# Head rows duplicated into both tile halves: one transfer with a repeated source in place of two

## What is computed

```python
def hybrid_layer(x, ...):                      # twice
    z = rms_norm(x, norm_g) @ w_in
    o_a = fox_attention(heads(fq, 4), heads(fk, 4), heads(fv, 4), ff + fox_b) * silu(f_gate)
    o_b = conformer_conv(...)
    o_c = nsa_attention(heads(nq, 8), ..., heads(nks, 2), heads(nvs, 2), heads(nkw, 2), heads(nvw, 2), ...)
    return x + concatenate([o_a, o_b, o_c]) @ w_out

def second_block(x, ...):                      # two layers
        h = rmsnorm(x, norm1_g[l]) @ w_in[l]
        y_a = gdn_mixer(a_qkv, a_z, a_ab, ...)
        y_b = diff_mixer(b_q, b_k, b_v, ...)   # s = q k^T per head of 64, softmax, a = p0 - lam * p1
        y_c = swa_mixer(c_q, c_k, c_v, ...)
        y_d = mlstm_mixer(d_q, d_k, d_v, d_if, d_o, ...)
        ...
```

## Time and profile before

| | |
|---|---|
| median of 3 runs | 4367.03 us (4355.88 to 4370.16) |
| the profiled execution | 4360.56 us, of which the span of the profile is 4358.8 us |
| TensorE matmul busy | 3567.8 us, 82% |
| VectorE busy | 2326.0 us, 53% |
| ScalarE busy | 1369.9 us, 31% |
| GpSimd busy | 580.0 us, 13% |
| mean granted TensorE clock | 0.886 of 2.4 GHz |
| moved by DMA | 375.23 MB, 86 GB/s on average |

### The profile page before, as it was taken

One profiled execution on the slowest core, in us unless ns is written; L12 is line 12 of the kernel. 1 busy time (PEld: TensorE's weight loads), 2 busy tenths in 40 slices (PEclk: granted clock), 3 DMA queues, 4 the chain that ended last, 5 costly groups with the idle time before them and its releaser, 6 DMA issues. The chain is left out here.

```text
span 4358.8 us, 48555 instructions
## 1 busy us (share of the span) xinstructions
PE 3567.8 (82%) x17648; PEld 2936.1 (67%) x17648; DVE 2326.0 (53%) x4358; ACT 1369.9 (31%) x2554; POOL 580.0 (13%) x450
## 2 busy tenths in 40 slices
PE   7857788577789998778378999879998775598997
PEld 6646676566567887556366888668886564477886
DVE  3366633656337775557464333357875556563333
ACT  2213421233223332333323322233333333323331
POOL 1000000000103332101101110013331001102110
PEclk9967899677889999898589999989999887699999
DMA  4331134301243322221243333342223221253332
GB/s 139 111 95 43 31 109 120 99 23 42 65 132 89 90 81 79 87 77 52 59 129 99 92 97 87 110 125 85 83 65 99 82 65 49 57 156 83 92 97 68
DMA packets 567443, 375.23 MB, mean 86 GB/s; under 512 B 74501, under 2 KB 498437, under 8 KB 566941
## 3 DMA queue, kind: packets, MB, share of 16 engines
q1 hardware_dynamic: 567196, 372.01, 29.8%
HBM read 313.94 MB, written 58.00 MB: 85 GB/s over the span
## 5 line engine op out<-in xcount | busy, mean ns | idle before, releaser
L817 PE MATMUL bank<-h,w_hi 128*128 128x512 f32 (+1 forms) x1264 | 567.1, 449 | 71.5 <-DVE w_low L860 54.5
L819 PE MATMUL bank<-h,w_low 128*128 128x512 f32 (+1 forms) x1264 | 515.0, 407 | 0.0
L818 PE MATMUL bank<-h,w_hi 128*128 128x512 f32 (+1 forms) x1264 | 514.6, 407 | 0.0
L455 DVE TENSOR_TENSOR w_low<-w,w_hi 128x1024 fp32r<-128x1024 f32 (+1 forms) x202 | 265.5, 1314 | 193.6 <-ACT w_hi L449 192.5
L449 ACT CAST w_hi<-w 128x1024 fp32r<-128x1024 f32 (+1 forms) x202 | 210.5, 1042 | 503.7 <-DMA w<-in_w_mlp 242.8
L817 PEld LDWEIGHTS bank<-h,w_hi 128*128 128x128 f32 (+1 forms) x1264 | 252.2, 200 | 140.0 <-DVE w_low L860 63.3
L311 PE MATMUL bank<-h,w_hi 128*128 128x512 f32 x752 | 301.3, 401 | 33.9 <-DVE w_low L951 30.7
L313 PE MATMUL bank<-h,w_low 128*128 128x512 f32 x752 | 297.5, 396 | 0.0
L818 PEld LDWEIGHTS bank<-h,w_hi 128*128 128x128 f32 (+1 forms) x1264 | 252.1, 199 | 57.0 <-issue 13.5
L819 PEld LDWEIGHTS bank<-h,w_low 128*128 128x128 f32 (+1 forms) x1264 | 248.9, 197 | 59.4
L312 PE MATMUL bank<-yT_low,w_hi 128*128 128x512 f32 x640 | 254.2, 397 | 0.0
(11 more groups left out here) (434 smaller groups left out, 7611.0 us busy)
## 6 DMA issues: line engine op xcount, KB each, us to landing
w<-in_w_in SPq DMA_DIRECT2D x148, 512.0 KB, 4.1
w<-in_w_mlp SPq DMA_DIRECT2D x128, 512.0 KB, 4.1
z<-z_tile SPq DMA_DIRECT2D x212, 256.0 KB, 2.3
w<-in_w_gate SPq DMA_DIRECT2D x64, 512.0 KB, 4.1
q_twice<-z SPq DMA_DIRECT2D x128, 128.0 KB, 2.8
w<-in_w_out SPq DMA_DIRECT2D x32, 512.0 KB, 4.0
w<-in_w_branch SPq DMA_DIRECT2D x64, 256.0 KB, 3.0
gate<-z SPq DMA_DIRECT2D x64, 256.0 KB, 2.9
```

The lines of the kernel that those rows point to most:

```text
L455: self.v.tensor_tensor(self.wl[s][:, :, 0:n], self.w[s][:, :, 0:n], self.wh[s][:, :, 0:n].bitcast(F32), ALU.subtract).then_inc(self.w_low. ...
L817: self.t.matmul(bank[0:n, :], wh, self.k.hH[:, j, :], start=j == 0, stop=False)
L818: self.t.matmul(bank[0:n, :], wh, self.k.hL[:, j, :], start=False, stop=False)
L819: m = self.t.matmul(bank[0:n, :], wl, self.k.hH[:, j, :], start=False, stop=j == KD - 1)
```

## The change

`twice` returns one pair in place of two: the destination is the whole tile of 128 rows, and the source is the 64 rows of z with a leading dimension of 2 whose step is zero. The program then carries one transfer per tile, whose source has the dimensions 2 x 64 x 512 and whose destination has 128 x 1 x 512. The semaphores count 16 per tile in place of 32. Each of the five stages issues through the new form; the order of all instructions on all engines is as before, with one transfer where two stood. Bytes written are the same, and so are bytes read.

```diff
 def twice(dst, src):
-    return (dst[0:HD, :], src), (dst[HD:P, :], src)
+
+    return dst[:, :], src.unsqueeze(0).to_broadcast([2, HD, T])
...
-        self.q_in, self.k_in = [[self.sig(f"{n}_in{h}", 2, by=32) for h in range(2)] for n in "qk"]
+        self.q_in, self.k_in = [[self.sig(f"{n}_in{h}", 2, by=16) for h in range(2)] for n in "qk"]
...
-                    for out, src in twice(x[h], z[at:at + HD, :]):
-                        s.dma_start(out, src).then_inc(landed[h].sem, 16)
+                    s.dma_start(*twice(x[h], z[at:at + HD, :])).then_inc(landed[h].sem, 16)
...
-        self.rows_in = [self.sig(f"rows_in{i}", 2, by=32) for i in range(6)]
+        self.rows_in = [self.sig(f"rows_in{i}", 2, by=16) for i in range(6)]
...
-                for out, src in twice(self.place(i)[0], z[at:at + HD, :]):
-                    s.dma_start(out, src).then_inc(self.rows_in[i].sem, 16)
+                s.dma_start(*twice(self.place(i)[0], z[at:at + HD, :])).then_inc(self.rows_in[i].sem, 16)
```

More of the change, by code:

```diff
@@ L2955, in __init__ @@
             self.sig(n) for n in ("lambda_difference", "lambda_made", "lambda_kept", "gain_made")]
-        self.rows_in = [self.sig(f"rows_in{i}", 2, by=32) for i in range(8)]
+        self.rows_in = [self.sig(f"rows_in{i}", 2, by=16) for i in range(8)]
         self.v_in = [self.sig(f"v_in{j}", 2, by=16) for j in range(2)]
@@ L3103, in __init__ @@
         self.table_in, self.sinks_in, self.negated = self.sig("rope_tables_in", by=16), self.sig("sinks_in", by=16), self.sig("sinks_negated")
-        self.rows_in = [self.sig(f"rows_in{i}", 2, by=32) for i in range(5)]
+        self.rows_in = [self.sig(f"rows_in{i}", 2, by=16) for i in range(5)]
         self.v_in, self.v_turned, self.v_copied = self.sig("v_in", 2, by=16), self.sig("v_turned", 2), self.sig("v_copied", 2)
@@ L3226, in __init__ @@
         self.gain_in, self.one_set = sig("gain_in", by=16), sig("one_set")
-        self.q_in, self.k_in = [[sig(f"{n}_in{h}", 2, by=32) for h in range(2)] for n in "qk"]
+        self.q_in, self.k_in = [[sig(f"{n}_in{h}", 2, by=16) for h in range(2)] for n in "qk"]
         self.v_in, self.o_in = [[sig(f"{n}_in{h}", 2, by=16) for h in range(2)] for n in "vo"]
```

## The result

The changed kernel takes 4722.62 us (median of 6 runs, 4714.73 to 4735.61), the kernel before 4367.23 us (6 runs). The ratio is 1.0821, with a 95% interval of 1.0802 to 1.0840: 355 us or 8.2% slower. The forecast was 4705, with a range of 4610 to 4900. The profiled execution has a span of 4719.7 us, where that of before has 4358.8.

A forecast was written before the change was run, and what follows sets the result against it. Head rows awaited at the 20 places where a mixer's pass begins were taken as the bound; their shifts, 67.5 + 103 = 170.5 us per layer of each stack, 341 for two, gave 4702 profiled, 4705 median, range 4610 to 4900.

The forecast's parts named there:

- Two engines per tile: Head-row transfers: an even share of the outermost counts 128 and 2 is possible on 2 engines only, inferred from 14 and 16.
- The price of a tile: Queue of the two engines: 5.5 us per tile plus 2.5 us fixed, so the last of n lands at 2.5 + 5.5 n.
- Place by place: The 20 places where a mixer's pass begins: shifts of 13 to 22 us, 170.5 us for one layer of each stack.
- Fox 1: Fox, first pass, four tiles: c_pair issued about 224.8 in place of 206.93, a shift of 18 us.
- The tail: From the last tile's landing to the start of L1839: 2.4 us, TensorE about 1.1 and the cosine 1.27.
- The clock after the waits: TensorE's first products after longer waits: more at granted clock 0.50, a microsecond or so a place, inside the range.
- Mlstm: Mlstm, second head's o rows: four tiles at 5.5 and four transfers at 0.7, a shift of 16 us in each pass.
- Diff: Diff, eight tiles and a weight tile: shifts of 22 us (19 to 27) in the first pass, 20 in the second.
- SP is never late: SP's issues: about 0.7 us saved per tile counts for nothing, since rows queue on two engines.
- The sum: Whole kernel: 170.5 us for one layer of each stack, 341 for two, so 4702 profiled and 4705 for a median.
- rival 3: Two engines at the crowded rate, 8.5 us a tile: 324 us on top, 5027; above 4900 given 4%.
- Rival 1: Transfer dealt by its destination stays on 16 engines: about 10 us saved per layer, 20 in all, 4341; 7%.

The follow-up runs named there:

- experiment 1: Changed kernel with the repetition moved inside, so the source's outermost count is 64: 4353.61 us against 4372.20 for the kernel before, ratio 0.9961.
- experiment 2: Changed kernel with outermost count 2 but no zero step, two overlapping different stretches of rows: 4730.32 us, ratio 1.0825 to the kernel before.
- experiment 3: Changed kernel with each tile's transfer bringing 32 rows four times, outermost count 4: 4464.93 us against 4372.20 for the kernel before.
- experiment 4: Changed kernel with each tile's transfer bringing 16 rows eight times, outermost count 8: 4403.72 us, 31.5 above the kernel before.
- experiment 9: Changed kernel with value, gate and o rows issued ahead of the head tiles: 4707.24 us, 342 above the kernel before.
- experiment 7: Kernel before with the new transfer only for the first tile of each of the 20 places: 4474.81 us, 109 above the kernel before.
- experiment 6: Kernel before with the new transfer only in the four places of Nsa: 4441.84 us against 4365.59, ratio 1.0164.
- experiment 11: Kernel before with heads adjacent in z merged into one transfer per tile half, 64 outermost: 4399.43 us against 4365.59, ratio 1.0076.
- experiment 5: Changed kernel with eight copies of 16 rows taken from eight overlapping, different stretches: 4395.15 us, 22 above the kernel before's 4373.17.
- experiment 8: Changed kernel with two transfers per tile, cut by columns into 1 KB rows, both on two engines: 4759.07 us, 386 above the kernel before.

## Why the prediction was right

**Two engines per tile.** The step inferred from 14 and 16 small packets held: 3241 fewer were seen, 3240 computed, and experiments 1 to 4 show one count moving packets, steps and time. The rule that the forecast named beside it, from the Trainium skill (DMA: Bandwidth & Descriptors, Why a DMA increments its semaphore by 16 and not by 1), agrees at outermost counts of 2, 4, 8 and 64, with 2, 4, 8 and 16 small packets a tile. Of the same page's Rules for kernel authors, the one that the prediction took up, on an outermost count below 16, is borne out; the leading zero-step dimension is its example, and experiment 2 shows that the count alone does it. The other rule, one transfer of 128 partitions in place of two for separate halves, holds only if that count isn't broken: followed with a count of 2 it cost 8.2%, and with 64 outermost (experiment 1) it gave 0.4%.

**The price of a tile.** I took 5.5 us, between 5.2 and 8.5, because 14 idle engines can't crowd two. Measured 5.35 in Nsa (5.55 with the long step), 5.26 in Mlstm with experiment 9's order, 5.0 to 5.4 in Diff. The uncrowded rate was the right choice; experiment 7 shows that the other one is real where the engines are busy.

**Place by place.** From the first issue to the instant that the earlier trace rows name, in us; "before" from those rows, "forecast" by the prediction's steps (the two Diff shifts hold 3 and 1.6 us for weights on top of the instant), "after" from the trace:

| place (first layer) | before | forecast | after | shift forecast | shift seen |
|---|---|---|---|---|---|
| Fox 1, c_pair issued | 8.7 | 26.6 | 25.2 | 18 | 16.5 |
| Fox 2, v rows read | 8.1 | 25.2 | 25.2 | 17 | 17.1 |
| Nsa 1, last add | 19.0 | 37.9 | 40.6 | 19 | 21.6 |
| Nsa 2, last add | 24.4 | 37.9 | 40.5 | 13.5 | 16.1 |
| Diff 1, last add | 30.8 | 49.9 | 52.1 | 22 | 21.3 |
| Diff 2, last add | 31.8 | 50.2 | 51.5 | 20 | 19.7 |
| Swa 1, last add | 20.2 | 33.4 | 35.3 | 13 | 15.1 |
| Swa 2, last add | 16.6 | 32.4 | 34.2 | 16 | 17.7 |
| Mlstm 1, second o rows | 11.0 | 27.3 | 29.2 | 16 | 18.2 |

**The tail** was mis-sized. From landing to the last add I counted 2.4 us. In Nsa it is 4.7: the last rotation starts at 416.42, and the last of these four is the add. VectorE:

```profile
418.53 0.69 DVE L1834 TENSOR_TENSOR rope_tmp<-bank,nsa_tables 128x512 f32<-128x512 f32 x1 [2.55 <-PE bank L1799]
419.14 1.25 DVE L1839 TENSOR_TENSOR q_twice<-q_twice,rope_tmp 128x512 f32<-128x512 f32 x1
420.43 0.69 DVE L1846 SCALAR_TENSOR_TENSOR q_stacked<-q_twice,q_stacked 64x512 fp32r<-64x512 f32 x1
421.15 0.69 DVE L1839 TENSOR_TENSOR q_twice<-q_twice,rope_tmp 128x512 f32<-128x512 f32 x1
```

Two things are in it. The first is the clock. I had taken a rotation of 1.1 us from the earlier trace rows; after waits the stretch has a granted clock of 0.52, close to 1.2 GHz, and a rotation takes 2.07, 1.0 us more:

```profile
380.00:420.00 40.00, 14.57 (x24) 5.24 (x24) 11.69 (x15) 2.75 (x5) 7.60 (x6) 0.52 0.18 60
```

The second is VectorE's order. Behind the rotation I had only the cosine, 1.27 us. But VectorE works one tile behind: after the last tile's sine product (L1834) come the add of the tile before and a remainder (L1846), and only then the last add, 2.6 us after the rotation's end. That is 1.3 us more, and it is there at the high clock too. In Swa's first pass the last rotation starts at 2174.86 and takes 1.13 us, and the last add still comes 3.8 us after that start:

```profile
2174.86 1.13 PE L1799 MATMUL bank<-q_twice,rope_tables 128*128 128x512 f32 x2 [1.12 <-DMA q_twice<-z]
...
2178.67 0.69 DVE L1839 TENSOR_TENSOR q_twice<-q_twice,rope_tmp 128x512 f32<-128x512 f32 x1
```

The landing itself was right: 416.42 less 380.60 is 35.8, forecast 35.5. That is partly luck, since the plain step was 5.35 and the long one made up the rest. The tail explains most of what Nsa and Swa took beyond the forecast (2.3 us, of 2.6 to 2.7, in Nsa; 1.4 us, of 1.9, in Swa's first pass; in its second 2.3, where the rest came 0.5 sooner), and with 2.3 us at each of four places most of the 11 us that experiment 6 found beyond 65.

**The clock after the waits.** "A microsecond or so a place" was more than most places show. Take the stretch from the last add to the next place's first issue, for the six places with rotations in the first layer. In Nsa's first pass it is 3.8 us longer than before. In the other five it is between 2.7 us shorter and 1.1 longer. The attention that follows had this before and now:

```profile
368.00:424.00 56.00, 54.41 (x398) 52.47 (x397) 38.08 (x152) 27.84 (x85) 0.00 (x0) 0.86 0.00 1
```

```profile
420.00:484.00 64.00, 58.98 (x399) 57.12 (x398) 42.41 (x156) 29.98 (x89) 0.00 (x0) 0.77 0.00 1
```

The first row is of before, the second of after: 398 matmuls and 399, with 4.6 us more of busy time at a clock of 0.77. In the second layer the same stretch, from the last add to the next issue, took 59.6 us after and 59.1 before, where the first layer has 63.0 and 59.1. Experiments 2 and 6 have it the other way round (59.1 and 62.9, 59.6 and 63.0), and experiment 9 has 61.8 in both. So some 4 to 5 us are paid by the two layers together, not always by the same one. Why, I can't say.

**Mlstm** was short by 2 us, probably for a queue that I left out: the four pair_R transfers ahead of the tiles still keep the engines busy after the first tile is issued at 2308.64, and the 2 us are all there when the first v rows are read:

```profile
2308.00:2310.00 2.00, 0.00 (x0) 0.00 (x0) 0.00 (x0) 0.00 (x0) 0.00 (x0) 0.50 0.73 245
2310.00:2312.00 2.00, 0.00 (x0) 0.00 (x0) 0.00 (x0) 0.00 (x0) 0.00 (x0) 0.50 0.49 174
```

**Fox 1** came 1.5 us short of the forecast. The four tiles and the v rows took 24.4 us in place of 25.2, and what lies behind them up to the issue of c_pair 0.8 in place of 1.4.

**Diff** was within 1 us by two errors that cancel. The last tile's rotation starts 44.4 us after the first issue, 3 us sooner than the 47.5 of the forecast, but the last add follows 7.7 us later and not 2.4. VectorE, first pass, shows why (its line L861 is the low part of a weight tile):

```profile
1932.57 1.23 DVE L861 TENSOR_TENSOR w_low<-w,w_hi 128x1024 fp32r<-128x1024 f32 x1 [6.07 <-ACT w_hi L832]
...
1935.74 0.69 DVE L1839 TENSOR_TENSOR q_twice<-q_twice,rope_tmp 128x512 f32<-128x512 f32 x1
```

and ScalarE, which rounds that tile before it:

```profile
1931.49 1.05 ACT L832 CAST w_hi<-w 128x1024 fp32r<-128x1024 f32 x1 [9.62 <-DMA w<-in_w_gate]
```

The weight tile stands behind the head tiles in the queue and lands 47.9 us after the first issue (forecast 51.0). It is what ends the wait here: the last two adds stand behind its low part in VectorE's order. Attention starts 5.5 us after the last add, as before, and 21.3 us later than before counted from the first issue. Of the 12.4 us between weight rounding and attention before, 9.8 are kept, which with the earlier landing gives 21.3 and not the 27 of the upper end.

**"SP is never late"** was right for the sum and wrong as a picture: SP was held at its issues. I take the stall for a consequence and not a second loss: experiment 7 loses 109 us without any, and what waits in SP would otherwise wait in the two engines' queue. No run has the one without the other at all 108 tiles.

**The sum.** The shifts seen, Mlstm's taken twice, make 181.5 us a pair of layers where 170.5 were forecast: 363 in all for 341. The whole profiled span grew by 361 (from the first place's issue to the twentieth's, so without the last place, by 342). So the way of reckoning, shifts of 20 instants added up, holds, and the 22 us that were missing are two terms: the tail in Nsa and Swa, about 17, and Mlstm's queue, about 8, less small change in Fox and Diff. Diff's agreement is luck, as said above. Two sums in the prediction are a little off: 4702 and 6.5 make 4708 and not 4705, from which the median measured is 14.5 us away and not 17.6, and rival 3's 4702 and 324 make 5026.

**The rivals.** Rival 1 is out (the small packets). Its price, -20, is near the -19 of experiment 1, but in that trace the 20 places add up to no gain at all, so the places that it was added up from are not shown, and the agreement may be luck. Rival 2 is out: tiles land one behind the other, 5.35 us apart. Rival 3 doesn't hold in this kernel, though its rate appears in experiment 7.

## What to carry to other kernels

Before merging transfers, look at the outermost count on both sides: it decides how many engines work, and a transfer that saves one issue of 0.6 us can cost 5 us of queue that everything behind it shares. Count the packets under 512 bytes per transfer to see it in a profile. Fewer transfers are not a goal in themselves: even on 16 engines, merged loads (experiment 11) lost 0.8%, and where the trace was read the first consumer waited for the last row. And where a loop works one step behind, as VectorE does here, what follows the last landing is longer than one tile's chain: count what stands ahead of the last operation in the engine's own order.

## What was not expected of the hardware

- The issuing engine is held back. The first two tiles leave SP in 0.5 to 0.6 us, the third in 2.8, the fourth in 5.2. From then on SP issues at the pace of the two engines, 5.0 us a tile in Diff. With four engines (experiment 3) the first three issues are short as well and the v rows' takes 1.75 us; with eight (experiment 4) none is long. So, as far as these three show, it goes by what is queued per engine.
- An engine's rate is not fixed. Two engines move 25 GB/s each, four 24.5 (98 GB/s together), eight 18.5 where all read the same rows and 23.4 where they read different ones (experiments 4 and 5, one window each). Two engines amid 14 busy ones fell to about 16 (experiment 7, worked out from the landing), and had 24.5 each again when the others were done.
- A tile in rows of 1 KB cost 10% more than in rows of 2 KB on a loaded engine, 8 ns a packet (experiment 8).
